# A two-layer decoder step on one core: last sums begun with transposing products, and waits and copies reordered

## What is computed

```python
def sq_relu_mlp(x, w_up, w_down):
    return jnp.square(jax.nn.relu(x @ w_up)) @ w_down
...
            h, (C, n, m) = mlstm_mixer(x, w_in_a[layer], b_gate_a[layer], w_out_a[layer], C0[layer], n0[layer], m0[layer])
...
            h = attend(q, ctx).reshape(B, L, QB_W) @ w_out_b[j]
        x = layer_norm(ALPHA * x + h, ln_g[layer, 0], ln_b[layer, 0])
        x = layer_norm(ALPHA * x + sq_relu_mlp(x, w_up[layer], w_down[layer]), ln_g[layer, 1], ln_b[layer, 1])
```

## Time and profile before

| | before |
|---|---|
| time, median of 3 runs | 921.65 us (921.1 to 924.53) |
| the profiled execution | 922.45 us |
| its span | 920.7 us |
| mean granted TensorE clock | 0.997 |
| TensorE busy | 905.9 us, 98% |
| VectorE, ScalarE, GpSimd busy | 624.3, 438.1, 55.7 us |
| moved by DMA | 182.77 MB, mean 199 GB/s |

### The profile page before, as it was taken

One profiled execution on the slowest core, in us unless ns is written; L12 is line 12 of the kernel. 1 busy time (PEld: TensorE's weight loads), 2 busy tenths in 40 slices (PEclk: granted clock), 3 DMA queues, 4 the chain that ended last, 5 costly groups with the idle time before them and its releaser, 6 DMA issues.

```text
span 920.7 us, 18778 instructions
## 1 busy us (share of the span) xinstructions
PE 905.9 (98%) x7509; PEld 842.8 (92%) x7509; DVE 624.3 (68%) x1097; ACT 438.1 (48%) x826; POOL 55.7 (6%) x71
## 2 busy tenths in 40 slices
PE   9999999999999999999999999999999999999996
PEld 8899988899999999998888878977999999999975
DVE  5467668778977475676575848446569797657526
ACT  5445666466345363445344453345547634536320
POOL 0010003500000000330000000000230000000000
PEclk9999999999999999999999999999999999999999
DMA  9963314664445444566988997998945455444301
GB/s 284 265 213 109 105 47 125 198 186 146 137 148 156 155 138 147 173 222 228 313 300 289 355 370 284 399 401 329 284 140 183 138 175 184 144 138 145 131 0 58
DMA packets 132331, 182.77 MB, mean 199 GB/s; under 512 B 5875, under 2 KB 113211, under 8 KB 132244
## 3 DMA queue, kind: packets, MB, share of 16 engines
q1 hardware_dynamic: 126938, 177.54, 58.6%
q10 hardware_dynamic: 4666, 1.92, 0.8%
q0 software_dynamic: 640, 2.10, 0.6%
HBM read 175.22 MB, written 6.32 MB: 197 GB/s over the span
## 4 chain that ended last, share of the span: by engine, by line
PE 92%; SPq 3%; DVE 2%; ACT 1%; DMA 1%; issue 1%; DVEq 0%
PE ps L621 23%; PE ps L623 23%; PE ps L622 22%; PE ps L985 6%; PE ps L1027 3%; PE ps L1085 3%; SPq L511 1%; DMA raw<-in_w_in_a_dram 1%; PE ps L873 1%; PE ps L875 1%; PE ps L874 1%; PE ps L863 1%; PE ps L635 1%; PE ps L738 0%; PE ps L882 0%
## 5 line engine op out<-in xcount | busy, mean ns | idle before, releaser
L1189 ACT ACTIVATE w_hi<-raw 128x1024 fp32r<-128x1024 f32 x192 | 202.6, 1057 | 246.1 <-PE ps L623 222.8
L1581 DVE TENSOR_TENSOR w_lo<-raw,w_hi 128x1024 fp32r<-128x1024 f32 x192 | 236.5, 1234 | 115.9 <-ACT w_hi L1189 115.6
L621 PE MATMUL ps<-x_hi,w_hi 128*128 128x322 f32 (+1 forms) x888 | 279.6, 315 | 2.3 <-ACT k_mlstm L1243 1.9
L623 PE MATMUL ps<-x_hi,w_lo 128*128 128x322 f32 (+1 forms) x888 | 276.2, 311 | 0.0
L622 PE MATMUL ps<-x_lo,w_hi 128*128 128x322 f32 (+1 forms) x888 | 275.9, 311 | 0.0
L621 PE MATMUL ps<-h_hi,w_hi 128*128 128x320 f32 x568 | 176.3, 310 | 0.7 <-DVE h_lo L1717 0.7
L623 PE MATMUL ps<-h_hi,w_lo 128*128 128x320 f32 x568 | 175.3, 309 | 0.0
L622 PE MATMUL ps<-h_lo,w_hi 128*128 128x320 f32 x568 | 175.3, 309 | 0.0
L621 PEld LDWEIGHTS ps<-x_hi,w_hi 128*128 128x128 f32 x888 | 167.9, 189 | 8.0 <-ACT k_turned L1479 2.9
L622 PEld LDWEIGHTS ps<-x_lo,w_hi 128*128 128x128 f32 x888 | 168.5, 190 | 0.2
L623 PEld LDWEIGHTS ps<-x_hi,w_lo 128*128 128x128 f32 x888 | 167.5, 189 | 0.0
(11 more groups left out here) (337 smaller groups left out, 962.6 us busy)
## 6 DMA issues: line engine op xcount, KB each, us to landing
raw<-in_w_up_dram SPq DMA_DIRECT2D x32, 1024.0 KB, 5.8
raw<-in_w_down_dram SPq DMA_DIRECT2D x32, 1024.0 KB, 5.2
page<-in_cache_k_dram SPq DMA_DIRECT2D x64, 512.0 KB, 5.5
page<-in_cache_v_dram SPq DMA_DIRECT2D x64, 512.0 KB, 8.9
raw<-in_w_in_a_dram SPq DMA_DIRECT2D x11, 1024.0 KB, 8.7
raw<-in_w_kv_dram SPq DMA_DIRECT2D x8, 1024.0 KB, 7.2
raw<-in_w_out_a_dram SPq DMA_DIRECT2D x4, 1024.0 KB, 5.3
raw<-in_w_q_b_dram SPq DMA_DIRECT2D x4, 1024.0 KB, 5.3
```

What stands on the lines that cost most here:

```text
L621: mm(out, WH[PLACE[t]][:, k, :], hi[:, k, 0:width], start=(k == 0), stop=False)
L623: last = mm(out, WL[PLACE[t]][:, k, :], hi[:, k, 0:width], start=False, stop=(k == 7))
L1189: A(WH[PLACE[t]][:, :, :], raw_tile(t), ACT.Copy)\
L1581: V.tensor_tensor(WL[PLACE[t]][:, :, :], raw_tile(t), WH[PLACE[t]][:, :, :].bitcast(F32), ALU.subtract)\
```

## The change

Tile 0 and 1 of the mixer's output are interleaved. The last quad begins with the prompt's chunks of X as transposing products, which start each bank's sum, and w_down's products are added on top; the samples' chunks are still added as products (`x_sample`). The prompt's and the samples' n are one product with 40 columns of weights, for which GpSimd folds the sum onto 64 partitions beside the sample rows. The second copy of the samples' V goes from VectorE to GpSimd. Unit 4 is loaded ahead of `C0`; some emptyings, copies, exponents and scalings change their place on ScalarE and VectorE, and the own products move from page 5 to page 1. Left out below: widths and indices of the layer-norm columns (64 to 48), of the base constants' load and the new semaphore `s_tvu`.

```diff
@@ -119,8 +119,9 @@
     n = np.tile(np.arange(4) + 1.0, (128, 2)).astype(np.float32)
-    bm = np.zeros((128, 8), np.float32)
-    bm[0:64] = (sb[:, None] == np.arange(NB)[None, :])
+    bm = np.zeros((128, 40), np.float32)
+    bm[64:128, 0] = 1
+    bm[0:64, 32:40] = (sb[:, None] == np.arange(NB)[None, :])
@@ -207,11 +208,11 @@
         SQ = put("xx", [128, T])
-        base = put("base", [128, 268])
-        ident, ones, bmask = base[:, 0:128], base[:, 128:256], base[:, 256:264]
-        bmask4 = base[:, 264:268]
-        lnT = put("ln_cols", [128, 64])
-        lnA = put("ln_cols_alpha", [128, 64])
+        base = put("base", [128, 300])
+        ident, ones, bmask = base[:, 0:128], base[:, 128:256], base[:, 256:296]
+        bmask4 = base[:, 296:300]
+        lnT = put("ln_cols", [128, 48])
+        lnA = put("ln_cols_alpha", [128, 48])
@@ -384,7 +386,7 @@
         SCORE_BANK = (4, 7, 5, 6)
-        OWN_BANK, TURN_BANK = (1, 0), ((2, 3, 2, 3), (2, 1, 3, 0))
+        OWN_BANK, TURN_BANK = (1, 0), ((2, 3, 2, 3), (2, 1, 0, 3))
@@ -506,11 +508,12 @@
             sp.dma_start(table[:, :], page_table.rearrange("b p -> (b p)").unsqueeze(0)).then_inc(s_tab, 16)
+            load_unit(4)
...
                                  state_C[0, :, 2 * j + h2].rearrange("b k v -> k b v")).then_inc(s_c0, 16)
-            for u in range(4, 7):
+            for u in range(5, 7):
@@ -807,11 +810,35 @@
-            def h_ready(k):
...
-                if k == 5:
-                    turned_back(7)
-                return s_hl, k + 1
+            def heads_out():
...
+                t = 8 * Q_WOA
...
+                def chunk(n, k):
+                    out, hi, lo = dense_bank(t + n)[:, 0:T], HH[0][:, k, 0:T], HL[0][:, k, 0:T]
+                    mm(out, WH[PLACE[t + n]][:, k, :], hi, start=(k == 0), stop=False)
+                    mm(out, WH[PLACE[t + n]][:, k, :], lo, start=False, stop=False)
+                    return mm(out, WL[PLACE[t + n]][:, k, :], hi, start=False, stop=(k == 7))
...
+                pe.wait_ge(*emptied(t - 2))
+                pe.wait_ge(s_lo, t + 1)
+                for k in range(7):
+                    if k == 5:
+                        turned_back(7)
+                    pe.wait_ge(s_hl, k + 1)
+                    chunk(0, k)
+                pe.wait_ge(*emptied(t - 1))
+                pe.wait_ge(s_lo, t + 2)
+                for k in range(3):
+                    chunk(1, k)
+                pe.wait_ge(s_hl, 8)
+                chunk(0, 7).then_inc(s_mm, 1)
+                state_step(1)
+                for k in range(3, 8):
+                    last = chunk(1, k)
+                last.then_inc(s_mm, 1)
+                state_step(2)
@@ -819,8 +846,9 @@
             turned_back(6)
-            for n in range(8):
-                dense(8 * Q_WOA + n, HH[0], HL[0], h_ready if n == 0 else None)
+            heads_out()
+            for n in range(2, 8):
+                dense(8 * Q_WOA + n, HH[0], HL[0])
@@ -832,9 +860,7 @@
                 pe.wait_ge(s_ws2, 1)
-                mm(ps[5][0:1, :], ones[:, 0:1], Wst[:, :], start=True, stop=True, skip_group_check=True)
-                mm(ps[5][32:40, :], bmask[0:64, :], wsK[0:64, 2, :], start=True, stop=True, skip_group_check=True)\
-                    .then_inc(s_np, 1)
+                mm(ps[5][0:40, :], bmask, wsK[:, 2, :], start=True, stop=True, skip_group_check=True).then_inc(s_np, 1)
@@ -858,10 +884,14 @@
                 c = slice(128 * (n % 4), 128 * (n % 4) + 128)
-                for i in range(3):
-                    tok = slice(128 * i, min(128 * i + 128, T))
-                    mm(summed(i, n // 4)[0:tok.stop - tok.start, c], X[:, n, tok], ident, start=False, stop=False,
-                       skip_group_check=True)
+                for i in range(2):
+                    mm(summed(i, n // 4)[:, c], X[:, n, 128 * i:128 * i + 128], ident, start=(n % 4 == 0), stop=False,
+                       is_transpose=True, skip_group_check=True)
...
+            def x_sample(n):
...
+                c = slice(128 * (n % 4), 128 * (n % 4) + 128)
+                mm(summed(2, n // 4)[0:64, c], X[:, n, TP:T], ident, start=False, stop=False, skip_group_check=True)
@@ -870,7 +900,7 @@
                 wh, wl = flat(WH[PLACE[t]], half), flat(WL[PLACE[t]], half)
-                mm(out, HH[1][:, k, tok], wh, start=(k == 0), stop=False, skip_group_check=True)
+                mm(out, HH[1][:, k, tok], wh, start=False, stop=False, skip_group_check=True)
@@ -891,17 +921,16 @@
                     pe.wait_ge(s_lo, t + k + 1)
-                    for i in range(2):
-                        for half in range(2):
+                    for half in range(2):
+                        if k == 0:
+                            for n in range(4 * half, 4 * half + 4):
+                                x_turn(n)
+                        for i in range(2):
                             down_prompt(k, i, half)
-                    if k == 0:
-                        pe.wait_ge(*emptied(t - 3))
                     down_sample(k).then_inc(s_mm, 1)
-                    for n in ((0, 1, 2), (3, 4), (5, 6))[k]:
-                        x_turn(n)
+                    for n in ((0, 1, 2), (3, 4, 5), (6, 7))[k]:
+                        x_sample(n)
                 for k in range(3, 8):
-                    if k == 7:
-                        x_turn(7)
@@ -1040,11 +1069,11 @@
                     if G == 1 and c < 3:
-                        pe.wait_ge(*((s_tv, 7), (s_uk, 24), (s_tv, 8))[c])
+                        pe.wait_ge(*((s_tv, 7), (s_uk, 24), (s_ptc, 6))[c])
                     if G == 0 and c >= 2:
-                        pe.wait_ge(s_ptc, c)
+                        pe.wait_ge(s_ptc, c - 1)
                     if G == 1 and c == 3:
-                        pe.wait_ge(s_ptc, 6)
+                        pe.wait_ge(s_tv, 8)
@@ -1059,8 +1088,8 @@
-                pe.wait_ge(s_ptc, 5 * G + 1)
-                pe.wait_ge(s_tv, 8)
+                pe.wait_ge(s_ptc, (5, 6)[G])
+                pe.wait_ge(s_tvu, 8)
@@ -1076,7 +1105,7 @@
                 if q == 0:
-                    pe.wait_ge(s_ptc, 5 * G + 5)
+                    pe.wait_ge(s_ptc, (4, 10)[G])
@@ -1089,7 +1118,7 @@
-                dense(8 * Q_WV + n, XH, XL, None, TW, (s_uk, 16 + n - 1) if n >= 2 else (s_ptc, 1))
+                dense(8 * Q_WV + n, XH, XL, None, TW, (s_uk, 16 + n - 1) if n >= 2 else (s_ptc, (1, 5)[n]))
@@ -1123,11 +1152,11 @@
             probs_turn(1)
-            pe.wait_ge(s_ptc, 8)
+            pe.wait_ge(s_ptc, 7)
...
                 page_values(1, q)
-                if q == 5:
+                if q == 1:
@@ -1233,14 +1262,14 @@
                 t = 8 * Q_QK + n
+                if n < 4:
+                    A(qT[:, n, :], tile(t), ACT.Copy).then_inc(s_ev[0], 1)
+                else:
+                    A(kT[:, n - 4, :], tile(t), ACT.Copy, scale=DK ** -0.5).then_inc(s_ev[0], 1)
...
                     rows_exp()
-                if n < 4:
-                    A(qT[:, n, :], tile(t), ACT.Copy).then_inc(s_ev[0], 1)
-                else:
-                    A(kT[:, n - 4, :], tile(t), ACT.Copy, scale=DK ** -0.5).then_inc(s_ev[0], 1)
@@ -1438,7 +1467,8 @@
                     rstd(1)
-                kvq(i)
+                if i < 7:
+                    kvq(i)
@@ -1506,14 +1536,18 @@
             def probs_copy(G):
-                act.wait_ge(s_ptt, 5 * G + 1)
-                for r in (slice(0, 64), slice(64, 128)):
-                    ins = A(PTo[G][r, :, :], ps[OWN_BANK[G]][0:64, 0:256].rearrange("p (a r) -> p a r", a=2), ACT.Copy)
-                ins.then_inc(s_ptc, 1)
-                for c in range(4):
-                    act.wait_ge(s_ptt, 5 * G + c + 2)
-                    A(PT[G][:, 4 * c:4 * c + 4, :], ps[TURN_BANK[G][c]][:, :].rearrange("p (m r) -> p m r", m=4),
-                      ACT.Copy).then_inc(s_ptc, 1)
...
+                for part in ((0, 1, 2, 3, "own"), ("own", 0, 1, 2, 3))[G]:
+                    if part == "own":
+                        act.wait_ge(s_ptt, 5 * G + 1)
+                        for r in (slice(0, 64), slice(64, 128)):
+                            ins = A(PTo[G][r, :, :], ps[OWN_BANK[G]][0:64, 0:256].rearrange("p (a r) -> p a r", a=2),
+                                    ACT.Copy)
+                        ins.then_inc(s_ptc, 1)
+                    else:
+                        act.wait_ge(s_ptt, 5 * G + part + 2)
+                        A(PT[G][:, 4 * part:4 * part + 4, :],
+                          ps[TURN_BANK[G][part]][:, :].rearrange("p (m r) -> p m r", m=4), ACT.Copy).then_inc(s_ptc, 1)
@@ -1526,6 +1560,8 @@
                 k_copy(P)
+                if P == 0:
+                    kvq(7)
@@ -1535,8 +1571,11 @@
                 split_to(min(8 * Q_WV + n + 2, 8 * Q_WV + 7))
+                if n == 7:
+                    exp_step(1, 8)
+                    exp_step(1, 9)
                 kvq(16 + n)
-                if n >= 3:
```

(33 more changed lines are left out.)

## The result

| | before | after |
|---|---|---|
| time, median of 6 runs each, same chip | 921.72 us (921.09 to 924.53) | 915.08 us (913.38 to 916.42) |
| ratio of the runs | | 0.9925, 95% interval 0.9909 to 0.9941 |
| span of the profiled execution | 920.7 us | 914.0 us |
| mean granted TensorE clock | 0.997 | 0.995 |
| last product of TensorE ends at | 913.60 us | 906.92 us |

What follows compares the result with a forecast made beforehand. TensorE was taken as the bound, busy 905.9 of 920.7 us. Terms summed to 9.85 us, giving 912.6 from the profiled 922.45 or 911.8 from the median; forecast 912.3, range 909.6 to 915.5.

Steps and rivals of the forecast that it cites:

- late pages: Rival, attention: page loads don't keep pace with the earlier start, the 2.2 shrinks to about 0.7, 913.8 us; chance 0.12.
- waits that move: Rival: several waits move as the mixer's does; only the products' saving and the 2.05 remain, 915.4 us; chance 0.10.
- The start, 2.1: Kernel start: unit 4's earlier load and reordered emptying remove waits of 2.05 and 0.55, a new 0.45 wait appears.
- The mixer's output, -0.3: Last head: interleaved tiles cover its 0.7 wait but delay the weighted keys; the wait moves, 0.3 lost, other end +0.9.
- first rival: Half-clock stretch at 48 to 51 us goes, 910.7 us, chance 0.15; or another such stretch, 913.9, chance 0.08.
- The prompt state, 0.95: Prompt's state: one of two products over 512 columns goes, 0.95 us gained; GpSimd's added work costs nothing.
- Pages, 0.8: First key pages: ScalarE's copy of the first turned page, put ahead of a scaling, removes a wait, 0.8 us gained.
- first probabilities, 0.3: First turned probabilities: own block's two copies go last, so the 0.6 wait shrinks, 0.3 us gained, ends 0 and 0.7.
- Second group and heads, 2.2: Second attention group and prompt's heads: bank order, moved own products, halved scalings gain 2.2 us, ends 1.2 and 2.4.
- The last sums, 3.8: Last quad: transposing products of one instruction a block take 3.8 us in place of 7.6; ends 3.2 and 4.3.
- third rival: Last sums: transposing products stay two instructions a block, sixteen times 0.11 us back, 914.1 us; chance 0.03.
- the fourth: Rival, last sums: transpose mode lets the clock fall to half, up to 19 us more, 931 us; chance 0.02.

Runs made afterwards that it cites:

- the repeated run: The changed kernel run again, unaltered, beside other kernels on the same chip: 914.71 us, ratio 0.9925 to the kernel before.
- the wait filled: Changed kernel plus eight products over 320 columns, never read, in TensorE's wait ahead of the first state products: 914.96 us, ratio 0.9929.
- the plain products: Changed kernel with the prompt's sixteen turned chunks of x as plain products by the identity instead of transposing ones: 918.08 us, ratio 0.9959.
- alone: Kernel before with only the attention's edits (page copy first, probabilities' order, banks, own products, halved scalings, GpSimd's copies): 919.59 us, ratio 0.9973.

## Why the prediction was right, and where not

The sign, the range and most terms held; the gain was 6.6 in place of 9.4. That the time fell inside the range, 0.4 from its end, is partly luck: the upper end was drawn for late pages and for waits that move, and it was filled in part by others, the fold beside VectorE and VectorE's chain among the heads. Of the signs that the prediction named, the product of 512 columns came at 177.7 instead of 175 and TensorE's last at 906.5 instead of 903.5. By its own steps:

**The start, 2.1** (its own terms add up to 2.15). At the states times q the changed kernel is 2.45 ahead (1.6 in the repeated run, whose wait for ln_cols was 1.4 instead of 0.6). The next unit's split was forecast to stay at 42.28 and started at 41.93, and what hangs from it followed (timelines of ScalarE, VectorE and TensorE):

```profile
41.93 1.06 ACT L1218 ACTIVATE w_hi<-raw 128x1024 fp32r<-128x1024 f32 x1 [3.31 <-DMA raw<-in_w_in_a_dram]
...
43.02 1.23 DVE L1620 TENSOR_TENSOR w_lo<-raw,w_hi 128x1024 fp32r<-128x1024 f32 x1 [5.75 <-ACT w_hi L1218]
...
44.40 0.20 DVE L1688 COPY ln_cols<-ps 128x48 f32<-128x48 f32 x1
...
44.66 0.42 PE L624 MATMUL ps<-x_hi,w_hi 128*128 128x320 f32 x1 [0.60 <-DVE ln_cols L1688]
```

ScalarE waits for the load; by its landing, with the split between 41.69 and 43.04, TensorE's new wait is 0.3 to 1.4 in seven profiled executions. The forecast had 0.4 to 0.5 and 1.4 as its end. In the two where TensorE comes 2 to 3 us later (the wait filled, the plain products) there is next to none.

**The mixer's output, -0.3.** The chain was read rightly: the wait moved to the first state products and the edit lost 0.15. What a wait of 1.3 can do to the clock stood only in the first rival ("another such stretch, 913.9", at 0.08). It happened in the profiled execution and costs 1.56; why it came is not shown.

**The prompt state, 0.95.** The step that failed is "GpSimd pays ... it costs nothing". The product gave 1.09, but the price was asked only of when the product is due (176 us), not of what GpSimd holds up beside it. The prediction even had the next chunk sum "under 1.1 late" and did not ask who waits for it. The addition was bounded by 1.31 and took 2.15, and the operations of VectorE grew by 0.36 and 1.03. What VectorE and GpSimd then deliver late are the last chunk sum and the low part of x, both on TensorE's path: 1.16 lost. The rows say which operations meet: w_lo and x_lo, which read two tiles of SBUF, are stretched and stretch GpSimd's addition; the additions to C, which read one operand from PSUM, take 2.14 to 2.15 beside it or not. The Trainium skill, in "SBUF — State Buffer", section "Who interferes with whom", has this as a rule: a VectorE instruction with two SBUF inputs contends with a GpSimd instruction that reads SBUF. The same page of the Trainium skill, section "SBUF: two separate sides", adds that whichever starts first gets the shared ports for its whole length. The trace agrees: in the changed kernel GpSimd's addition, drawn from 160.34, ends 1.15 after w_lo does (162.49 and 161.34), and x_lo, drawn from 161.26, ends at 162.84, 0.35 after that addition.

**Pages, 0.8, and first probabilities, 0.3.** 0.74 and 0.34, alone 0.87 and 0.27.

**Second group and heads, 2.2.** 2.20 at the first rows turned back, then 0.80 returned before the third layer norm. The forecast capped this term by the loads of pages, and these were in time. The cap was VectorE: its chain of scores, maxima and scalings, with low parts of w between, was about 3.2 us ahead of before at that point while TensorE was 4.0, and the waits for p_stats (0.3) and p_logit (0.5) are the difference made up. From VectorE's timeline:

```profile
620.83 0.55 DVE L1988 SCALAR_TENSOR_TENSOR p_logit<-attn_tables,ps 128x384 f32<-128x384 f32 x1
...
624.03 1.23 DVE L1620 TENSOR_TENSOR w_lo<-raw,w_hi 128x1024 fp32r<-128x1024 f32 x1 [0.20 <-ACT w_hi L1218]
```

The first of these was at 624.01 in the kernel before:

```profile
624.01 0.55 DVE L1946 SCALAR_TENSOR_TENSOR p_logit<-attn_tables,ps 128x384 f32<-128x384 f32 x1
```

That VectorE's chain is the cause is read from such rows; no run took work off it.

**The last sums, 3.8.** 3.5. From start to start, the groups of x take 3.76 in place of 7.61, so 3.85 as priced; the w_down products between them take 30.4 in place of 30.1, for a reason that I did not trace. (At 0.97 a chunk the groups before would be 7.7; the prediction wrote 7.6, and that is what they take.) The third rival (no cheaper) is refuted by the plain products, the fourth (a clock that falls) by a granted clock of 1.00 from 870 to 900. The rule of the Trainium skill, "TensorE: Matmul & The Clock Gate", Part 4, that transpose mode doesn't count as busy for the clock, was not seen at work here.

In sum, of 9.85 forecast the profile shows 6.68, and with the 1.56 of the second slow stretch 8.24. The missing 1.6 is the fold's 1.16, the heads' 0.80 and the last sums' 0.28, less 0.35 and 0.15 that the start and the mixer's output did better and 0.12 in the three small terms.

## What to carry to other kernels

Before work is put on an idle GpSimd, look at what VectorE does in those microseconds: where VectorE read two tiles of SBUF the two held each other up here, and the price falls on whatever waits for VectorE, so put such work beside VectorE's reads of PSUM: there the addition on 64 partitions took 1.27. When a wait moves instead of going, ask which later step could move with it: one tile of delay for four state products was worth 2.35 here, where the edit that brought their wait lost 0.15.

## What was not expected of the hardware

Slow stretches of clock do not fall in the same places in each execution of one kernel: between 42 and 53 us in 13 of 14, at the start (8 to 16 us) in three profiled ones of one chip, at 140 us only where TensorE stood idle 1.3 us just ahead, and there not always. Most last 3.4 us, three about 6.8; the one at 140 us costs 1.5 to 1.6, with TensorE the bound (104.72, and 104.70 with the plain products, against 103.16), which is more than most single edits here, so that an edit's worth is better read between landmarks than from medians. And an addition on 64 partitions took 1.27 or 2.15 us on GpSimd, by its neighbour alone.
